# Recurrent entry on the unscaled sum, projections scaled by a row as their banks are read, and first units by part

## The chip, the cores and the metric

The kernel runs on one core of one Trainium2 chip. A core has TensorE (PE, which multiplies matrices into eight PSUM banks), ScalarE (ACT), VectorE (DVE), GpSimd (POOL) and SyncE (SP, which issues most transfers here). The metric is the device time of one execution, in microseconds (us). Times with a start are counted from the start of the profiled span.

## What is computed

A token block x of 256 tokens with 1024 features, in float32, goes through nine residual stages: feed-forward, the recurrent mixer ("even"), feed-forward, feed-forward, latent attention ("mla"), feed-forward, feed-forward, forgetting attention ("fox"), feed-forward. Each stage normalises x and adds its result to it. Cut to the parts that the change touches:

```
def _rmsnorm(x, gain):                     # x * rsqrt(mean(x*x)) * gain
def _swiglu(h, w_gate, w_up, w_down):      # D_FF = 2816
    return (silu(h @ w_gate) * (h @ w_up)) @ w_down
def _conv_rwkv_mixer(h, ...):              # stage 1, "even"
    p = h @ w_in                           # 3*512 conv columns, 3*512 + 32 + 32 + 96 recurrent ones
    gate_b, gate_c, h_in = split(p_conv)
    y_conv = gate_b * short_conv(gate_c * h_in, conv_w)          # 3 taps
    p_rwkv = p_rwkv + (shift(p_rwkv) - p_rwkv) * mu_shift        # the token before, mixed in
    r, k, v, dw, da, dg = split(p_rwkv)
    log_w = -softplus(-(w0 + tanh(dw) @ w_up)) - 0.5             # decay
    a = sigmoid(a0 + da @ a_up);  g = sigmoid(dg) @ g_up
    kk = normalised per head(k * k_k)
    y = scan over tokens: S = S*decay + (S@-kk)(kk*a) + v k ;  y_t = S@r_t
    y = group norm of y, bonus, times g
    return concat(y_conv, y) @ w_out
x = x + 0.5 * _swiglu(_rmsnorm(x, g[0]), ...)   # a feed-forward stage
x = x + mixer(_rmsnorm(x, g[1]))
```

## The kernel before

Every float32 operand of a product is split into a high part (rounded by a cast) and a low part (the rest), and a product is the sum of three: high by high, high by low, low by high (`three_products`, L385). Weights come from memory as units: `raw_gu` (1 MB) and `raw_dn` (0.5 MB). ACT makes the high parts (`hi_gu` L351, `hi_dn` L361), DVE or POOL the low parts (`lo_gu` L365, `lo_dn` L371, `lo_dn_pool` L378). A feed-forward stage has 22 units, the recurrent stage 12. Each engine's order is written out by hand; engines meet at semaphores, in the recurrent stage through `after(engine, other, step)`, which waits until the other engine has done the named step.

**An ordinary seam** (into stages 3, 5, 6, 8). DVE adds a stage's result to x in four quarters (L500). PE transposes the unscaled x (`gained_pe`, L456), ACT reads the banks scaled by the norm's gain into `h_hi` (L414), DVE makes `h_lo` (L442). The first unit runs on these: first the gate's column block by part of h, in the order `SEAM` (L399, L400 for high parts, L575 for low ones), then the up block with three products (L385). ACT squares x (L426, first half ahead of `h_hi`, second half behind it), takes the inverse root (L432, L435), DVE turns it into two diagonals (L465), PE multiplies them by ones into a bank (L474), ACT copies that: `rstd_row`, one factor per token in each column, by which gate and up are later scaled.

**The recurrent stage** is another thing at its entry: ACT squares x by quarters (L1019), POOL and ACT make the inverse root (L974, L1025 to L1037), DVE scales x by it (L1219), and only then PE transposes (L1414). So its 26 projection tiles (`tile(i)`, each 128 or 96 columns by 256 tokens, in three units' pieces) come out of their banks ready. For tiles 0 to 13, which are mixed with the token before, ACT reads the bank scaled by 1 - mu (`evac(i)`, L989) and DVE then adds mu times the bank shifted by a token (`mix(i)`, L1192). Tiles 14 to 25 are copied by ACT (`evac(i)`, L992): 14 to 17 are v, 18 to 25 the convolution's.

The chain of the stage: tiles 0 to 3 (k), their squares (L1048) and the key norm (PE L1445, DVE L1237, ACT L1060); tile 4 and 5 (low rank); tanh and two low-rank products (PE L1535, L1539), the gate's sigmoid (L1066), the decay's sigmoid (L1069) and the other one (`iclr`, L1072); the cumulative sum of the decays (PE L1547); kk, b, their scaled forms (DVE L1245 to L1254); key scores on PE (L1461); five levels of products that invert the chunk triangles (the first is PE L1505 at 246.63 us); states and outputs; group norm; the output products (`row` by `row`, L385, whose left operand is `h_both` from `conv_hi` L1152 and `conv_lo` L1378 for the convolution's half, with `y_conv` L1375 ahead).

Of the kernel before, what the change touches and what calls it, by code (L numbers as in the profile page):

```python
# [10 lines left out]
ALU = mybir.AluOpType  # L11
# [236 lines left out]
def build(nc, units_gu, units_dn, x_in, positions, constants, params, low_rank, final_gain, out, stages=STAGES):  # L248
# [6 lines left out]
    with ExitStack() as ctx:  # L255
# [30 lines left out]
        rstd_row = arena[:, 17, T:2 * T]  # L286
        banks = ctx.enter_context(nc.psum_tensor("banks", [P, 8, 512], F32))
# [37 lines left out]
        x_ready, stored = sem("x_ready"), sem("stored")  # L325
        first_gate_landed, first_gate = [sem("first_gate_landed_0"), sem("first_gate_landed_1")], sem("first_gate")
# [64 lines left out]
        SEAM = (("hi", 0), ("hi", 1), ("hi", 2), ("lo", 0), ("hi", 3), ("lo", 1), ("lo", 2), ("lo", 3))  # L391

# [5 lines left out]
        def high_products(out, w, h, first):  # L398
            nc.tensor.matmul(out, w[0], h, start=first, stop=False)  # L399
            return nc.tensor.matmul(out, w[1], h, start=False, stop=False)  # L400

# [65 lines left out]

        def rstd_row_pe(pe, s):

            if s == 0:  # L470
                pe.wait_ge(ones_loaded, 16)
            pe.wait_ge(diag_ready, ffn_index(s) + 1)
            for t in range(2):
                ins = nc.tensor.matmul(banks[:, 7, t * P:(t + 1) * P], const("ones"), rstd_diag[:, t, :], start=True, stop=True)  # L474
            ins.then_inc(row_summed, 1)

        def rstd_row_act(act, s):
            act.wait_ge(row_summed, ffn_index(s) + 1)
            nc.scalar.copy(rstd_row, banks[:, 7, 0:T]).then_inc(row_ready, 1)

        def ffn_index(s):
            return sum(k == "ffn" for k in stages[:s])
# [44 lines left out]
        FIRST_UP_BANK = 5  # L527
# [32 lines left out]
        def ffn_first_up(pe, s):  # L560
# [4 lines left out]
            gate, up = banks[:, bank, 0:T], banks[:, FIRST_UP_BANK if s == 0 else bank, T:2 * T]  # L565
# [29 lines left out]
            for part, b in SEAM:  # L595
                gate_part(part, b)
            for k in range(KD):
                w = slice((KD + k) * P, (KD + k + 1) * P)
                ins = three_products(up, (gu_hi[:, 0, w], gu_lo[:, 0, w]), (h_hi[:, k, :], h_lo[:, k, :]),
                                     k == 0, k == KD - 1)  # L600
            ins.then_inc(gu_used, 1)
# [102 lines left out]
        def ffn_all_act(act, s):  # L704
# [13 lines left out]
            else:  # L718
# [21 lines left out]
        def ffn_all_dve(dve, s):  # L740
# [24 lines left out]
            ffn_dve(dve, b, 0, f, True, None, seam_bank(s), FIRST_UP_BANK if s == 0 else None)  # L765
# [95 lines left out]
        def even_names():  # L861
# [9 lines left out]
            act = [("square_x", 0), ("square_x", 1), "ln_x0", "rstd_x0"] + evac(0, 4) + ["square_k"] + evac(4, 5) + ["ln_k"] + evac(5, 6) + ["tanh", "gate_sig"] + evac(6, 7)  # L871
            act += ["decay_sig", "iclr", "inv_k"] + evac(7, 8) + ["e0", "em", "e1", "mid", "factor", "gate"] + evac(8, 10)
            act += halves("m", -1) + evac(10, 11)
            for l in range(NL):
                act += ([("tok", TOKS[l])] if l < 3 else []) + [("mt", l)]
                act += (halves("m", l) if l < NL - 1 else []) + ["a_crossed"] * (l == 0) + evac(11 + l, 12 + l)
            act += [("tok", "v")] + evac(16, 17) + ["g"] + evac(17, 18) + ["uw"] + evac(18, 19) + ["phi"] + evac(19, 21) + ["y0"]
            act += evac(21, 24) + ["square_y"] + evac(24, 25) + ["ln_y"] + [("conv_hi", j) for j in range(3)] + ["rstd_y"]
            act += evac(25, 26) + [("conv_hi", 3)] + [("y_hi", j) for j in range(4)]
            mix = lambda a, b: [("mix", i) for i in range(a, b)]  # L880
            dve = [("scaled", t, c) for t in range(2) for c in range(2)] + ["omu", "omka"] + mix(0, 5) + ["one_row", "key_ss"] + mix(5, 8) + ["kkn", "b", "at", "bt"]
            dve += ["mt0", "mt1"] + mix(8, 9) + ["kh", "ab0", "ab", "kt"] + mix(9, 11)
            for l in range(NL):
                dve += halves("x", l) + ["ak"] * (l == 3) + [("mt", l)] + (["rt", "ec"], ["bonus"], [], [], ["rk"])[l]
                dve += mix(11 + l, 12 + l) if l < 3 else []
            conv = lambda j: [(n, j) for n in ("u", "tap0", "tap1", "tap2")]
            state = lambda n: [("sd", n), ("sum", n), ("s", n)]
            dve += ["rb", "bv", "bv_b", "uw", "s1"] + conv(0) + [("q", 0), ("q", 1)] + state(1) + [("y", 1)]
            dve += conv(1) + state(2) + [("y", 2)] + conv(2) + [("y", 3)] + conv(3) + ["centred"]
            dve += [("y_conv", j) for j in range(3)] + [("conv_lo", j) for j in range(3)] + [("y_conv", 3), ("conv_lo", 3)]  # L890
# [3 lines left out]
            pool = [("bias_x", 0), ("bias_x", 1), "pads"]  # L894
# [21 lines left out]
        x_ss, x_bias = mla_stats[:, 16:20], mla_stats[:, 20:22]  # L916
        x_scaled = [arena[:, slot, 0:D] for slot in (RC, VC)]
# [45 lines left out]

        def mix_column(i):
# [5 lines left out]
        def even_pool(pool, s):  # L970
            done = EV["pool"].done
            for t in range(2):
                after(pool, "act", ("square_x", t))
                done(nc.gpsimd.tensor_scalar(x_bias[:, t:t + 1], x_ss[:, 2 * t:2 * t + 1], 1.0 / D, NORM_EPS, ALU.mult, ALU.add),  # L974
                     ("bias_x", t))
# [3 lines left out]
        def even_act(act, s):  # L979
# [5 lines left out]
            def evac(i):  # L985
                after(act, "pe", ("tile", i))
                if i < MIXED:
                    m = 96 if i in LOW_TILES else P
                    ins = nc.scalar.activation(tile_target(i), tile_place(i), ACT.Copy,  # L989
# [2154 lines left out]
```

## Time and profile before

| what | value |
|---|---|
| median of 3 runs | 1494.03 us (1493.0 to 1494.61) |
| profiled execution, its own time | 1492.92 us |
| its span from first to last instruction | 1491.1 us |
| granted TensorE clock, mean | 0.999 |
| PE / weight loads / DVE / ACT / POOL busy | 99 / 86 / 67 / 57 / 34 % |
| recurrent stage, in the trace | from about 194 to about 354 us |

"Busy" is the share of the span in which an engine had an instruction under way; where matmuls overlap each other they are counted once, so 99% of PE doesn't say how fast it works. A wait of PE is told with the line that waited and the line that released it; these few waits, and the place of each in the program, are what an edit on another engine can shorten or lengthen.

### The profile page before, as it was taken

How to read it: one execution, taken by the hardware profiler on the slowest of the kernel's cores; microseconds unless marked ns; L12 is line 12 of the kernel's file. 1: busy time of each engine (PE TensorE's matmuls, PEld its weight loads, DVE VectorE, ACT ScalarE, POOL GpSimd, SP SyncE). 2: the span in 40 equal slices, each digit the busy share in tenths (PEclk: the TensorE clock that was granted, in tenths of full speed). 3: DMA queues.
4: the chain of work that ended last, by engine and by line, in shares of the span. 5: the costliest groups of instructions: out<-in, count | busy, mean ns of one | idle time of the engine just before them, and what ended most of it. 6: DMA issues, size and time to landing. Idle time of an engine off the chain costs nothing. (4 is left out here: it accounts for less than half of the span.)

```text
span 1491.1 us, 25605 instructions
## 1 busy us (share of the span) xinstructions
PE 1469.7 (99%) x9520; PEld 1275.5 (86%) x9520; DVE 1002.2 (67%) x1303; ACT 854.2 (57%) x1316; POOL 508.1 (34%) x207
## 2 busy tenths in 40 slices
PE   8999999999999999999999999999999999999998
PEld 7888889898888888888988888888888887888886
DVE  6776567568775567765665777557765589877654
ACT  5555576446555565555676555555555678655544
POOL 2444400001444335443441344334444300144442
PEclk9999999999999999999999999999999999999999
DMA  7655542235555545555533555545655453265552
GB/s 258 225 206 195 185 141 74 101 115 176 205 197 187 200 154 193 199 189 202 184 114 113 183 197 187 206 156 189 207 192 190 169 198 113 100 211 186 205 184 87
DMA packets 48812, 259.99 MB, mean 174 GB/s; under 512 B 5584, under 2 KB 5968, under 8 KB 28144
## 3 DMA queue, kind: packets, MB, share of 16 engines
q1 hardware_dynamic: 29520, 190.49, 36.1%
q10 hardware_dynamic: 19152, 68.53, 13.8%
q8 instruction: 42, 0.69, 0.2%
q14 instruction: 18, 0.15, 0.0%
q0 software_dynamic: 80, 0.14, 0.0%
HBM read 258.08 MB, written 1.05 MB: 174 GB/s over the span
## 5 line engine op out<-in xcount | busy, mean ns | idle before, releaser
L378 POOL TENSOR_TENSOR dn_lo<-raw_dn,dn_hi 128x1024 fp32r<-128x1024 f32 x138 | 472.6, 3425 | 837.5 <-ACT dn_hi L361 828.6
L365 DVE TENSOR_TENSOR gu_lo<-raw_gu,gu_hi 128x2048 fp32r<-128x2048 f32 x161 | 369.3, 2294 | 181.8 <-ACT gu_hi L351 180.1
L606 PE MATMUL banks<-h_both,gu_hi 128*128 128x512 f32 x2016 | 478.1, 389 | 0.0
L606 PEld LDWEIGHTS banks<-h_both,gu_hi 128*128 128x128 f32 x2016 | 378.0, 188 | 78.2
L351 ACT CAST gu_hi<-raw_gu 128x2048 fp32r<-128x2048 f32 x160 | 304.9, 1906 | 12.0 <-PE banks L385 12.0
L613 PEld LDWEIGHTS banks<-h_both,gu_lo 128*128 128x128 f32 x2016 | 258.5, 191 | 9.8
L613 PE MATMUL banks<-h_both,gu_lo 128*128 128x256 f32 x2016 | 261.5, 283 | 0.0
L385 PE MATMUL banks<-dn_hi,act_hi 128*128 128x512 f32 x528 | 207.3, 393 | 0.5 <-DVE act_lo L555 0.5
L385 PE MATMUL banks<-dn_lo,act_hi 128*128 128x512 f32 x528 | 207.0, 392 | 0.0
L385 PE MATMUL banks<-dn_hi,act_lo 128*128 128x512 f32 x528 | 205.5, 389 | 0.0
L547 DVE TENSOR_TENSOR silu<-silu,arena 128x256 f32<-128x256 f32 x126 | 175.2, 1391 | 4.3
L361 ACT CAST dn_hi<-raw_dn 128x1024 fp32r<-128x1024 f32 (+1 forms) x162 | 167.8, 1036 | 7.0 <-DMA raw_dn<-units_dn 3.7
L521 ACT ACTIVATE silu<-silu 128x256 f32<-128x256 f32 x132 | 55.2, 418 | 168.6 <-DVE silu L547 168.1
L517 ACT COPY arena<-banks 128x256 f32<-128x256 f32 x126 | 46.7, 371 | 177.8 <-PE banks L613 177.5
L544 DVE TENSOR_TENSOR silu<-banks,arena 128x256 f32<-128x256 f32 x126 | 53.1, 422 | 98.8 <-ACT arena L517 98.7
L385 PEld LDWEIGHTS banks<-dn_hi,act_lo 128*128 128x128 f32 x528 | 99.2, 188 | 21.8
L385 PEld LDWEIGHTS banks<-dn_hi,act_hi 128*128 128x128 f32 x528 | 99.6, 189 | 18.5 <-POOL dn_lo L378 0.7
L385 PEld LDWEIGHTS banks<-dn_lo,act_hi 128*128 128x128 f32 x528 | 99.7, 189 | 15.7
L555 DVE TENSOR_TENSOR act_lo<-act,act_hi 128x256 fp32r<-128x256 f32 x132 | 62.7, 475 | 62.4 <-ACT act_hi L523 62.4
L523 ACT CAST act_hi<-act 128x256 fp32r<-128x256 f32 x132 | 53.6, 406 | 71.3 <-DVE act L553 68.4
L385 PE MATMUL banks<-gu_hi,h_both 128*128 128x512 f32 (+2 forms) x292 | 92.7, 384 | 0.2
L519 ACT COPY arena<-banks 128x256 f32<-128x256 f32 x126 | 47.0, 373 | 62.3 <-PE banks L613 61.7
(386 smaller groups left out, 1562.7 us busy)
## 6 DMA issues: line engine op xcount, KB each, us to landing
raw_gu<-units_gu SPq DMA_DIRECT2D x161, 1024.0 KB, 4.8
raw_dn<-units_dn ACTq DMA_DIRECT2D x130, 512.0 KB, 3.5
raw_dn<-units_dn SPq DMA_DIRECT2D x32, 512.0 KB, 3.4
x<-x_in SPq DMA_DIRECT2D x2, 512.0 KB, 4.9
cst<-constants SPq DMA_DIRECT2D x1, 688.0 KB, 6.0
raw_gu<-units_gu SPq DMA_DIRECT2D x2, 256.0 KB, 6.3
raw_gu<-units_gu SPq DMA_DIRECT2D x1, 512.0 KB, 7.5
lora<-low_rank SPq DMA_DIRECT2D x1, 512.0 KB, 7.2
```

What stands on the lines that cost most here:

```text
L351: nc.scalar.copy(gu_hi[:, p, :], raw_gu[:, p, :]).then_inc(gu_hi_ready, 1)
L361: nc.scalar.copy(dn_hi[:, p, 0:n], raw_dn[:, p, 0:n]).then_inc(dn_hi_ready, 1)
L365: nc.vector.tensor_tensor(gu_lo[:, p, :], raw_gu[:, p, :], gu_hi[:, p, :].bitcast(F32), ALU.subtract).then_inc(gu_lo_ready, 1)
L378: nc.gpsimd.tensor_tensor(dn_lo[:, p, 0:n], raw_dn[:, p, 0:n], dn_hi[:, p, 0:n].bitcast(F32), ALU.subtract).then_inc(dn_lo_ready, 1)
L385: ins = nc.tensor.matmul(out, a, b, start=first and i == 0, stop=last and i == 2)
L521: nc.scalar.activation(silu[:, p, :], silu[:, p, :], ACT.Silu).then_inc(silu_ready, 1)
L523: nc.scalar.copy(act_hi[:, p, :], act32[:, p, :]).then_inc(act_hi_ready, 1)
L544: nc.vector.tensor_tensor(silu[:, p, :], banks[:, 2 * p, 0:T], lo_half[:, p, 0, :], ALU.add).then_inc(halves_added, 1)
L547: nc.vector.tensor_tensor(silu[:, p, :], silu[:, p, :], rstd_row, ALU.mult).then_inc(gate_ready, 1)
L555: nc.vector.tensor_tensor(act_lo[:, p, :], act32[:, p, :], act_hi[:, p, :].bitcast(F32), ALU.subtract).then_inc(act_lo_ready, 1)
L606: ins = nc.tensor.matmul(banks[:, 2 * p + side, :], gu_hi[:, p, w], h_both[:, k, :, :].rearrange("p i t -> p (i t)"), start=k == 0, stop=F ...
L613: ins = nc.tensor.matmul(banks[:, 2 * p + side, 0:T], gu_lo[:, p, w], h_hi[:, k, :], start=False, stop=k == KD - 1)
```

## The change

1. At the start DVE writes zeros into a slot, and PE runs nine 128x128 float32 products on them before its first wait for a transfer.
2. In the recurrent stage the scaling of x goes. `gained_pe` transposes the unscaled sum as at an ordinary seam; ACT's squares and root stand behind `h_hi`, and `rstd_row_pe` and `rstd_row_act` make the row (in bank 3, copied to a free slot, `even_row`). A new DVE step, `raw(i)`, reads each tile's bank times the row. Tiles 14 to 25 are done with that. For tiles 0 to 13 `evac` and `mix` now read what `raw` wrote. Twelve ACT copies and three POOL instructions go; 26 DVE instructions come.
3. ACT's cast `hi_gu` of unit 3 moves from behind `evac(7)` to right behind the gate's sigmoid and ahead of `evac(6)`; DVE's `lo_gu` of unit 3 moves from behind `bt` to ahead of `raw(6)`. `kh` stands earlier on DVE, `mix(10)` behind the first level's masks, `raw(24)` and `raw(25)` ahead of `y_conv`.
4. First units of stages 2, 3, 5, 6 and 8, and tiles 0 and 1 of the recurrent stage, go gate and up together, by part of h (`both_by_part`), up in a bank of its own. ACT does all of `h_hi` first, then both squares.

```diff
+        def both_by_part(pe, s, outs, w, summed=None):
+            for part in ("hi", "lo"):
+                for b in range(4):
+                    for k in part_of_h(pe, s, part, b):
+                        for side, out_ in enumerate(outs):
+                            weights = w((side * KD + k) * P)
+                            if part == "hi":
+                                high_products(out_, weights, h_hi[:, k, :], k == 0)
+                            else:
+                                ins = nc.tensor.matmul(out_, weights[0], h_lo[:, k, :], start=False, stop=k == KD - 1)
...
+            both_by_part(pe, s, (gate, up), lambda a: (gu_hi[:, 0, a:a + P], gu_lo[:, 0, a:a + P])).then_inc(gu_used, 1)
...
-                squares_act(act, s, 0, loaded=stages[s - 1] in ("mla", "fox"))
                 h_hi_act(act, s)
-                squares_act(act, s, 1)
+                for t in range(2):
+                    squares_act(act, s, t, loaded=True)
                 inverse_root_act(act, s)
...
             def evac(i):
-                after(act, "pe", ("tile", i))
-                if i < MIXED:
...
-                else:
-                    ins = cp(tile_target(i), tile_place(i))
+                after(act, "dve", ("raw", i))
+                m = 96 if i in LOW_TILES else P
+                done(nc.scalar.activation(tile_target(i), unmixed(i), ACT.Copy,
+                                          scale=omu[0:m, mix_column(i):mix_column(i) + 1]), ("evac", i))
...
             h_hi_act(act, s)
-            nc.scalar.preload_act_table(ACT.Ln)
+            for t in range(2):
+                squares_act(act, s, t, loaded=True)
+            inverse_root_act(act, s)
             hi_gu(act, *unit(s, 1))
+            rstd_row_act(act, s)
...
             done(nc.scalar.activation(low(0, GATE_RANK, 1), low(0, GATE_RANK, 1), ACT.Sigmoid), "gate_sig")
+            hi_gu(act, *unit(s, 3))
             evac(6)
             after(act, "pe", "decay_in")
...
+            def raw(i):
+                after(dve, "pe", ("tile", i))
+                place = tile_place(i)
+                done(tt(unmixed(i) if i < MIXED else tile_target(i), place, even_row[0:place.shape[0], :], ALU.mult), ("raw", i))
+
             def mix(i):
                 after(dve, "act", ("evac", i))
-                done(stt(out=dst[:, 1:T], in0=tile_place(i)[:, 0:T - 1], scalar=pcol("mu", mix_column(i), m), in1=dst[:, 1:T],
+                done(stt(out=dst[:, 1:T], in0=unmixed(i)[:, 0:T - 1], scalar=pcol("mu", mix_column(i), m), in1=dst[:, 1:T],
...
+            raw(5)
             mix(5)
             lo_dn(dve, *unit(s, 2))
+            lo_gu(dve, *unit(s, 3))
+            raw(6)
+            raw(7)
             mix(6)
             mix(7)
...
             lo_gu(dve, *unit(s, 9))
+            raw(24)
+            raw(25)
             for some in ((0, 1, 2), (3,)):
                 for j in some:
-                    after(dve, "act", ("evac", 22 + j))
                     own(("tap2", j))
+                    own(("raw", 22 + j))
                     done(tt(c4(YC)[:, j, :], c4(CB)[:, j, :], c4(CC)[:, j, :], ALU.mult), ("y_conv", j))
...
+            both_by_part(pe, s, (tile_place(0), tile_place(1)), lambda a: w(a, P), lambda ins: done(ins, ("tile", 0))
+                         ).then_inc(gu_used, 1)
+            tile(2)
+            rstd_row_pe(pe, s)
+            tile(3)
+            tile(4)
             after(pe, "act", "square_k")
...
+            nc.vector.memset(arena[:, 0, 0:2 * P], 0.0).then_inc(zeros_ready, 1)
...
+            pe.wait_ge(zeros_ready, 1)
+            for i in range(9):
+                nc.tensor.matmul(banks[:, 3, 0:P], arena[:, 0, 0:P], arena[:, 0, P:2 * P], start=True, stop=True)
             pe.wait_ge(ident_loaded, 16)
```

ACT's order in the recurrent stage, from the table for the gate's sigmoid to the cast of unit 3, before (L1066 is the gate's sigmoid, L1069 the decay's, L1072 `iclr`, L1077 the inverse norm):

```order
L1061 ACT_TABLE_LOAD
L989 ACTIVATE act<-banks,mla_stats 96x256
L1064 ACTIVATE act<-act 32x256
L1066 ACTIVATE act<-act 96x256
L989 ACTIVATE arena<-banks,mla_stats 128x256
L1069 ACTIVATE arena<-banks 128x1024
L1072 ACTIVATE arena<-banks,par 128x256 x4
L1075 ACT_TABLE_LOAD
L1077 ACTIVATE arena<-arena,eps_col 128x1024
L989 ACTIVATE arena<-banks,mla_stats 128x256
L351 CAST gu_hi<-raw_gu 128x2048
```

and after the change (L1057 the gate's sigmoid, L1061 the decay's, L1064 `iclr`):

```order
L1052 ACT_TABLE_LOAD
L1001 ACTIVATE act<-arena,mla_stats 96x256
L1055 ACTIVATE act<-act 32x256
L1057 ACTIVATE act<-act 96x256
L353 CAST gu_hi<-raw_gu 128x2048
L1001 ACTIVATE arena<-arena,mla_stats 128x256
L1061 ACTIVATE arena<-banks 128x1024
L1064 ACTIVATE arena<-banks,par 128x256 x4
```

The cast of unit 3 stood behind the last of them and now stands between the two sigmoids; the bank reads have become reads of the arena.

DVE's order from the key norm's maximum (L1237) to the first masks of key scores (L1196), before:

```order
L1237 TENSOR_SCALAR arena<-banks 128x1024
L1192 SCALAR_TENSOR_TENSOR act<-banks,par,act 96x255
L371 TENSOR_TENSOR dn_lo<-raw_dn,dn_hi 128x1024
L1192 SCALAR_TENSOR_TENSOR arena<-banks,par,arena 128x255 x2
L1245 SCALAR_TENSOR_TENSOR arena<-arena,par 128x256 x4
L1249 TENSOR_TENSOR arena<-arena 128x1024
L1251 SCALAR_TENSOR_TENSOR arena<-arena 128x1024
L1254 TENSOR_TENSOR arena<-arena 128x1024
L365 TENSOR_TENSOR gu_lo<-raw_gu,gu_hi 128x2048
L1196 TENSOR_TENSOR arena<-banks,cst 128x1024
```

and after (L1222 the maximum, L1174 `raw`, L1179 `mix`, L1183 the masks):

```order
L1222 TENSOR_SCALAR arena<-banks 128x1024
L1174 TENSOR_TENSOR arena<-banks,silu 96x256
L1179 SCALAR_TENSOR_TENSOR act<-arena,par,act 96x255
L373 TENSOR_TENSOR dn_lo<-raw_dn,dn_hi 128x1024
L367 TENSOR_TENSOR gu_lo<-raw_gu,gu_hi 128x2048
L1174 TENSOR_TENSOR arena<-banks,silu 128x256 x2
L1179 SCALAR_TENSOR_TENSOR arena<-arena,par 128x255 x2
L1234 SCALAR_TENSOR_TENSOR arena<-arena,par 128x256 x4
L1238 TENSOR_TENSOR arena<-arena 128x1024
L1240 SCALAR_TENSOR_TENSOR arena<-arena 128x1024
L1243 TENSOR_TENSOR arena<-arena 128x1024
L1245 TENSOR_TENSOR arena<-arena 128x1024
```

The low split of unit 3 now stands ahead of `raw(6)` and `raw(7)`, and `kh` (L1245) has come in front of the masks.

DVE's order at the end of the stage, before (L1368 centres the group norm, L1375 `y_conv`, L1378 `conv_lo`):

```order
L1368 SCALAR_TENSOR_TENSOR arena<-banks,arena 128x1024
L365 TENSOR_TENSOR gu_lo<-raw_gu,gu_hi 128x2048
L1375 TENSOR_TENSOR arena<-arena 128x256 x3
L1378 TENSOR_TENSOR h_both<-arena,h_both 128x256 x3
L1375 TENSOR_TENSOR arena<-arena 128x256
```

and after (L1376, L1385, L1388):

```order
L1376 SCALAR_TENSOR_TENSOR arena<-banks,arena 128x1024
L367 TENSOR_TENSOR gu_lo<-raw_gu,gu_hi 128x2048
L1174 TENSOR_TENSOR arena<-banks,silu 128x256 x2
L1385 TENSOR_TENSOR arena<-arena 128x256 x3
L1388 TENSOR_TENSOR h_both<-arena,h_both 128x256 x3
L1385 TENSOR_TENSOR arena<-arena 128x256
```

The two reads of tiles 24 and 25, which ACT did, stand ahead of `y_conv`.

## Rows read from the trace of the kernel before

**Rows 1.** The page, part 1: busy us (share), instructions.
```profile
PE 1469.7 (99%) x9520; PEld 1275.5 (86%) x9520; DVE 1002.2 (67%) x1303; ACT 854.2 (57%) x1316; POOL 508.1 (34%) x207
```

**Rows 2.** PE's waits: us in total, times, longest.
```profile
PE banks L1505 <- issue: 1.7, 1, 1.7
...
PE banks L385 <- DVE dn_lo L371: 0.2, 1, 0.2
```

**Rows 3.** Line L456, 0 to 10 us: ns min/median/max, first and last start.
```profile
L456 PE MATMUL banks<-cst,x x16: 421/421/476, 5.4 to 8.6; 128*128 128x128 f32 x16
```

**Rows 4.** Line L456, 190 to 1300 us.
```profile
L456 PE MATMUL banks<-cst,x x112: 270/273/330, 354.2 to 1299.9; 128*128 128x128 f32 x112
```

**Rows 5.** Timeline of the start (start us, us, instruction, [idle before]).
```profile
5.39 3.68 PE L456 MATMUL banks<-cst,x 128*128 128x128 f32 x16 [5.39 <-DMA cst<-constants]
...
7.91 3.03 ACT L414 ACTIVATE h_both<-banks,par 128x256 fp32r<-128x256 f32 x8 [4.96 <-PE banks L456]
...
22.07 0.19 PEld L385 LDWEIGHTS banks<-dn_hi,act_hi 128*128 128x128 f32 x1 [0.65 <-POOL dn_lo L378]
```

**Rows 6.** Timeline of PE at the recurrent stage's entry.
```profile
193.19 0.39 PE L385 MATMUL banks<-dn_hi,act_lo 128*128 128x512 f32 x1
...
195.63 2.13 PE L1414 MATMUL banks<-cst,arena 128*128 128x128 f32 x16 [2.05 <-DVE arena L1219]
...
198.13 0.35 PE L399 MATMUL banks<-h_both,gu_hi 128*128 128x256 f32 x1 [0.37 <-ACT h_both L414]
```

**Rows 7.** Timeline of PE and DVE at the seam into stage 3.
```profile
540.24 2.06 PE L456 MATMUL banks<-cst,x 128*128 128x128 f32 x16
...
542.06 0.36 PE L399 MATMUL banks<-h_both,gu_hi 128*128 128x256 f32 x1
542.26 0.28 PE L400 MATMUL banks<-h_both,gu_lo 128*128 128x256 f32 x1
542.38 0.28 PE L399 MATMUL banks<-h_both,gu_hi 128*128 128x256 f32 x1
...
547.31 0.47 DVE L465 TENSOR_SCALAR arena<-cst,rstd 128x128 f32<-128x128 f32 x2
...
548.39 0.61 PE L474 MATMUL banks<-arena,cst 128*128 128x128 f32 x4
```

**Rows 8.** Groups of lines, 190 to 354 us: busy us, mean ns | idle before.
```profile
L365 DVE TENSOR_TENSOR gu_lo<-raw_gu,gu_hi 128x2048 fp32r<-128x2048 f32 x12 | 27.4, 2285 | 2.9 <-ACT gu_hi L351 2.9
...
L989 ACT ACTIVATE arena<-banks,mla_stats 128x256 f32<-128x256 f32 x12 | 5.7, 476 | 6.9 <-PE banks L385 6.9
L1192 DVE SCALAR_TENSOR_TENSOR arena<-banks,par,arena 128x255 f32<-128x255 f32 x12 | 5.7, 479 | 11.4 <-ACT arena L989 11.4
...
L992 ACT COPY arena<-banks 128x256 f32<-128x256 f32 x12 | 4.5, 371 | 22.3 <-PE banks L385 22.2
```

**Rows 9.** Timeline: a DVE product of a bank and the row, first stage.
```profile
18.79 0.42 DVE L538 TENSOR_TENSOR silu<-banks,arena 128x256 f32<-128x256 f32 x1
```

**Rows 10.** Timeline of PE: key norm, low-rank product, cumulative sum.
```profile
213.10 1.88 PE L1445 MATMUL banks<-arena,cst 128*128 128x512 f32 x4
...
220.60 0.69 PE L1535 MATMUL banks<-lora,act 64*128 64x512 f32 x1
...
225.50 3.61 PE L1547 MATMUL banks<-cst,arena 128*128 128x256 f32 x16
```

**Rows 11.** Timeline of ACT: decay sigmoid, cast of unit 3.
```profile
222.62 1.03 ACT L1069 ACTIVATE arena<-banks 128x1024 f32<-128x1024 f32 x1 [1.44 <-PE banks L1539]
...
227.82 1.89 ACT L351 CAST gu_hi<-raw_gu 128x2048 fp32r<-128x2048 f32 x1
```

**Rows 12.** Timeline: first level; end of the recurrent stage, DVE and PE.
```profile
246.63 1.16 PE L1505 MATMUL banks<-arena 64*64 64x64 f32 x64 [0.61 <-DVE arena L1206]
...
331.57 1.09 DVE L1378 TENSOR_TENSOR h_both<-arena,h_both 128x256 fp32r<-128x256 f32 x3 [2.04 <-ACT h_both L1152]
...
332.37 0.40 PE L385 MATMUL banks<-dn_hi,h_both 128*128 128x512 f32 x1
```

More of the change, by code:

```diff
@@ L478, in rstd_row_act @@
             act.wait_ge(row_summed, ffn_index(s) + 1)
[L479 removed]
+            nc.scalar.copy(even_row if stages[s] == "even" else rstd_row, banks[:, row_bank(s), 0:T]).then_inc(row_ready, 1)
         def ffn_index(s):
[L482 removed]
+            return sum(k in ("ffn", "even") for k in stages[:s])
         def add_to_x(dve, s):
@@ L875, in even_names @@
                 act += ([("tok", TOKS[l])] if l < 3 else []) + [("mt", l)]
[L876 to L879, printed above, removed]
+                act += (halves("m", l) if l < NL - 1 else []) + ["a_crossed"] * (l == 0) + (evac(11 + l, 12 + l) if l < 3 else [])
@@ L880, in even_names @@
+            act += [("tok", "v"), "g", "uw", "phi", "y0", "square_y", "ln_y"] + [("conv_hi", j) for j in range(3)] + ["rstd_y"]
+            act += [("conv_hi", 3)] + [("y_hi", j) for j in range(4)]
             mix = lambda a, b: [("mix", i) for i in range(a, b)]
-            dve = [("scaled", t, c) for t in range(2) for c in range(2)] + ["omu", "omka"] + mix(0, 5) + ["one_row", "key_ss"] + mix(5, 8) + ["kkn", "b", "at", "bt"]
-            dve += ["mt0", "mt1"] + mix(8, 9) + ["kh", "ab0", "ab", "kt"] + mix(9, 11)
+            raw = lambda *places: [("raw", i) for i in places]
@@ L891, in even_names @@
+            dve += [("q", 0), ("q", 1)] + state(1) + raw(20) + [("y", 1)]
+            dve += conv(1) + state(2) + raw(21) + [("y", 2)] + conv(2) + raw(22) + [("y", 3)] + conv(3) + raw(23) + ["centred"]
+            dve += raw(24, 25) + [("y_conv", j) for j in range(3)] + [("conv_lo", j) for j in range(3)] + [("y_conv", 3), ("conv_lo", 3)]
             for j in range(4):
@@ L1078, in even_act @@
             evac(7)
-            hi_gu(act, *unit(s, 3))
             after(act, "pe", "cumsum")
@@ L1254, in even_dve @@
             done(tt(flat(BT_), flat(BT_), flat(EM), ALU.mult), "bt")
-            lo_gu(dve, *unit(s, 3))
+            after(dve, "act", "factor")
+            done(tt(flat(KH), flat(KC), flat(AI), ALU.mult), "kh")
+            raw(8)
             after(dve, "pe", "ab")
@@ L1271, in even_dve, with raw_and_mix @@
             lo_dn(dve, *unit(s, 3))
-            mix(10)
-            level(0)
+            def raw_and_mix(i):
+                raw(i)
+                mix(i)
+            level(0, lambda: raw_and_mix(10))
             own(("mix", 9))
@@ L1296, in even_dve, with lo_and_raw @@
             level(3, ak)
-            level(4, lambda: lo_dn(dve, *unit(s, 5)))
+            def lo_and_raw():
+                lo_dn(dve, *unit(s, 5))
+                raw(14)
+            level(4, lo_and_raw)
             after(dve, "pe", "rk")
@@ L1336, in convolution @@
                 u, y = u_conv[:, j, :], c4(CC)[:, j, :]
-                after(dve, "act", ("evac", 18 + j))
+                own(("raw", 18 + j))
                 done(tt(u[:, 2:258], y, u[:, 2:258], ALU.mult), ("u", j))
@@ L1423, in tile @@
                 if ks[0] == 0 and i >= 6:
-                    after(pe, *(("dve", ("mix", i - 2)) if i - 2 < MIXED else ("act", ("evac", i - 2))))
+                    after(pe, "dve", ("raw", i - 2))
                 m = 96 if i in LOW_TILES else P
```

137 lines of the change are left out of this document (45 added, 92 removed).

## Prediction

> **What bounds the kernel now.** I began with the page: TensorE (PE) is busy for 1469.7 of 1491.1 us [rows 1]. An edit elsewhere can only pay if PE waits for that work, and costs if it makes PE wait. So the next view is PE's own waits [rows 2], then PE's timeline at the places the diff touches: the start [rows 5], the entry of the recurrent stage [rows 6], an ordinary first unit [rows 7], the joins inside the recurrent stage [rows 10, 12] and its end [rows 12]. For each place I ask which engine delivers last before and after.
>
> **What a step costs here.** In the recurrent stage, 190 to 354 us: one scaled bank read on ACT 0.476 us, one mix on DVE 0.479, one plain bank copy on ACT 0.371, one low split of a whole unit on DVE 2.29 [rows 8]. The new DVE instruction, a bank times a row, 128x256, has a twin in the feed-forward stage: 0.42 us [rows 9]. Twenty-six of them are 10.9 us of DVE; the twelve ACT copies that go are 4.5 us. Neither sum is the answer, since DVE and ACT idle before most of these. A 256-column matmul comes every 0.12 us (542.26, 542.38 [rows 7]); this is how I turn counts into time (estimate; 48 of them, 5.76 us).
>
> The Trainium skill, page "VectorE: DVE Perf Modes", section "Specifications", says that VectorE sits closer to SBUF and ScalarE closer to PSUM, which speaks against moving these bank reads. The rows give 0.42 against 0.371 us for the same shape; the trace agrees in direction, by 0.05 us. By the page alone no sum could be made.
>
> **Part 1, zeros at the start.** PE is idle for 5.39 us and then does 16 transposes at 421 ns each [rows 3, 5]; the same instruction is 273 ns later in the program [rows 4], and starts every 0.115 us rather than 0.23 us (3.68 us for 16 against 2.06 [rows 5, 7]). The nine matmuls fit into the idle 5.39 us. If they bring the later rate, the last transpose is some 1.6 us earlier, and ACT's h_hi (7.91) some 1 us. What follows does not follow: the gate's low weights and DVE's h_lo stand behind DVE's own splits. What can profit is ACT's chain to PE's first down product, before which the weight load waits 0.65 us [rows 5]. I take -0.4, bounds 0 and -0.65.
>
> The Trainium skill, page "TensorE: Matmul & The Clock Gate", section "Part 4: PE-mode transpose", says that the full clock does not engage for transposes. By that rule the 16 would stay as they are and this term would be 0. The trace speaks against it: the granted clock is given as full in both places, yet 421 ns and 273 ns stand for the same instruction.
>
> **Part 2, entry of the recurrent stage.** Before, the last down product starts at 193.19, PE waits 2.05 us for the scaled x, transposes from 195.63, and starts the first tile at 198.13 [rows 6]. After, the entry is like an ordinary seam: there transposes follow the last product at once, and the first product comes 1.82 us after the first transpose [rows 7]. Counted from 193.42 (0.23 behind the start of the last product, the pace of 512 columns), that is 195.24: 2.9 us gained, and taking tiles 0 and 1 together saves some 0.6 of small waits for h parts. It does not last, because the row must now exist before any tile leaves its bank. The low split of unit 1 (2.29, behind h_lo, a down split and the diagonals) ends at about 204.3 on DVE, an estimate, the row's matmuls and its copy give the row at about 204.85. From there the chain to the key norm is raw 0 and 1, evac 1, mix 1, a down split, raw 2, evac 2, a gate-up cast on ACT, evac 3, mix 3, a square: 0.84 + 0.48 + 0.48 + 1.2 + 0.42 + 0.48 + 1.9 + 0.48 + 0.48 + 0.5 = 7.3, with ten hand-overs 0.5 more: 212.65, against 213.10 before [rows 10]. PE, being early, waits there about 2.6 us. Then low split 2.29, raw 4, evac 4, mix 4, the norm's maximum, the table, evac 5 and tanh bring the low-rank product to 220.8, before 220.60 [rows 10]. **Entry gain 0.**
>
> **Part 3, the split moved behind the gate.** ACT before: gate sigmoid, evac 6, decay sigmoid at 222.62, and the cast hi_gu(3) only at 227.82 [rows 11]. After, hi_gu(3) stands right behind the gate sigmoid: from about 221.0 to 223.1. DVE then does lo_gu(3), 2.29 us, to 225.5, and only then raw 6, 0.42, which evac 6 on ACT waits for. The decay sigmoid stands behind evac 6 in ACT's order although its own input is ready by then: evac 6 at 225.9, the sigmoid 0.35 behind its start as ACT's instructions overlap, 226.25 instead of 222.62. The inverse root and evac 7 move with it, and so do the kk products of DVE. The cumulative sum on PE starts at 225.50 before [rows 10], some 0.4 after its input; after, at 228.76: **+3.26**, of which PE shows about 3.05 as one wait. The key scores come 3.6 later, as their chain has no such 0.4. PE's later waits of 0.2 and 0.61 us [rows 2, 12] go, since DVE had the time: the first level product moves from 246.63 to 249.4, **+2.75** in all. DVE has lost the split of 2.29 from behind bt, so it is not the bound.
>
> In the levels, raw, evac and mix stand in a row where evac and mix stood: 0.42 more in a chain that PE mostly covers by weight products; I take **+0.2** over three levels (0 to 1.26, all three in full).
>
> **Part 4, end of the stage.** Before, the three y_conv lie ready, conv_lo starts on DVE at 331.57 and PE goes from tile 25 into the row product at 332.37 [rows 12]. After, DVE must read tile 25 from its bank (raw 25) before the y_conv. Tile 25 ends at 332.37; then raw 0.42, a y_conv (DVE takes 1.09 for three of this shape [rows 12]), conv_hi, conv_lo: the row product at about 334.45, **+2.1**. ACT's evac 24 and 25 go, but ACT was not late. Bounds: 0.4 (a row product needs only j = 0 to start, and PE finds other work) and 2.6.
>
> **Part 5, ordinary first units.** Transposes at 540.24, first product 542.06, 48 products until the row's matmuls start at 548.39 [rows 7]: 0.57 us above 48 x 0.12. By part, PE has eight products for each 0.76 us in which ACT makes a pair of h_hi, so it is not starved. But the row also waits for DVE's diagonals, 547.31 to 547.78 [rows 7]. Both give 547.8: **-0.55** for each of stages 3, 5, 6 and 8, -2.2 in all (bounds: 0, if the diagonals slip as the squares now stand behind h_hi, to -2.4). For stage 2, behind the recurrent stage, ACT's second cast decides; I take -0.1 (0 to -0.55). ACT's squares and root move behind h_hi; they are covered by DVE's low split up to 547.3, and cost up to the 1.1 us of one square if that cover is gone.
>
> **Sum.** -0.4 + 0 + 2.75 + 0.2 + 2.1 - 2.2 - 0.1 = +2.35 us. The profiled execution took 1492.9 us, so 1495.3; the median of the runs shown is 1494.03, 1.1 above it, so **1496.4 us**.
>
> **Rivals.**
> (A) Forecast, likeliest, own range +0.4 to +3.8: chance 0.52.
> (B) PE's 1.7 us of "issue" at L1505 [rows 2], in which it waits for nothing that the profile shows, goes with the moved instructions, for their number before it changes. For: it is a place, not a dependency. Against: levels have the same instructions after. +0.65, 1494.7: 0.13.
> (C) The two new waits, 2.6 and 3.05 us, slow PE afterwards as the 5.4 us did at the start, 1.84 us for 16 transposes. For: rows 3. Against: the 2.05 us wait at 195.63 did not; 16 transposes took 2.13 us [rows 6], and 3.05 is nearer to it than to 5.39. It would add about 1.9: 1498.3, slower: 0.12. It decides if a wait of 3 us is enough.
> (D) The other side: DVE and ACT are ahead at the gate. Were raw 6 ready before hi_gu(3) matters, or the entry's lead kept through the key norm, then of the +2.75 at most 0.3 stays; and were raw 25 covered by remaining weight products, +0.4 in place of 2.1. Then -0.4 + 0.3 + 0.2 + 0.4 - 2.3 = -1.8, and with half of the entry's 3.5 kept, about -3.6: 1490.5, faster. For: 2.9 us are gained at the entry. Against: ACT's order puts the decay sigmoid behind evac 6. 0.12.
> (E) Both chains cost more: levels 1.26, end 2.6, seams 0. +2.35 + 1.1 + 0.5 + 2.2 = +6.1: 1500.1, slower: 0.11.
>
> **Range and chances.** 0.2% (3.0 us) is about what a measurement can tell from no change. From 1492.2 to 1499.2 holds A, B, most of C and the nearer part of D. Faster 0.12 (D), same 0.60 (most of A, B, a part of D), slower 0.28 (C, E and A's upper end).
>
> **What would show it.** In the trace after: a PE wait at the key norm of some 2.6 us and one before the cumulative sum of some 3, the latter released by ACT's iclr with DVE's lo_gu and raw 6 before evac 6; a PE wait of about 2 us behind tile 25 for h_both; transposes at the start of 270 to 330 ns; the row's matmuls 0.5 us sooner at the seams. I am wrong if the low-rank product comes well before 220 us, if tiles leave their banks before the row exists, or if the seams show new waits for the diagonals.

## The result, and the profile after

The changed kernel takes 1497.18 us (median of 14 executions, 1495.18 to 1499.94), the one before 1493.72 us (1492.40 to 1494.61). The ratio is 1.0026 (95% interval 1.0017 to 1.0034): slower by a quarter of a per cent, 3.5 us between the medians and 3.9 by the ratio. The predicted time was 1496.4 us. The profiled execution of the changed kernel took 1498.03 us, 0.85 above its median. Three single executions in the experiments below (5188.03, 3457.8 and 1614.11 us) lie far outside the others of their kernels and are left out of every median, range and ratio.

PE's waits in the changed kernel (us in total, times, longest):

```profile
PE banks L1447 <- ACT arena L1039: 2.6, 1, 2.6
PE banks L1545 <- ACT arena L1064: 2.2, 1, 2.2
PE banks L387 <- DVE h_both L1388: 1.9, 1, 1.9
PE banks L3106 <- DVE arena L3091: 1.2, 1, 1.2
...
PE banks L1507 <- issue: 0.7, 1, 0.7
```

The first three are new waits in the recurrent stage: the key norm, the cumulative sum, and the output products behind tile 25. They are those that the prediction named, with 2.6, 3.05 and about 2. The fourth is PE's wait at the start for DVE's zeros. The "issue" wait of [rows 2] is 0.7 instead of 1.7.

Timeline of the changed kernel at the gate, ACT, DVE and PE, and PE's first output product:

```profile
221.13 1.88 ACT L353 CAST gu_hi<-raw_gu 128x2048 fp32r<-128x2048 f32 x1
...
223.04 2.29 DVE L367 TENSOR_TENSOR gu_lo<-raw_gu,gu_hi 128x2048 fp32r<-128x2048 f32 x1 [1.14 <-ACT gu_hi L353]
...
225.25 0.42 DVE L1174 TENSOR_TENSOR arena<-banks,silu 128x256 f32<-128x256 f32 x1
...
225.71 0.51 ACT L1001 ACTIVATE arena<-arena,mla_stats 128x256 f32<-128x256 f32 x1 [2.69 <-DVE arena L1174]
...
226.12 1.00 ACT L1061 ACTIVATE arena<-banks 128x1024 f32<-128x1024 f32 x1
...
228.63 5.41 PE L1545 MATMUL banks<-cst,arena 128*128 128x256 f32 x16 [2.22 <-ACT arena L1064]
...
337.70 0.50 PE L387 MATMUL banks<-dn_hi,h_both 128*128 128x512 f32 x1 [1.85 <-DVE h_both L1388]
```

Read from top to bottom it is a chain: cast of unit 3, its low split, the read of tile 6, evac 6, the decay's sigmoid at 226.12 (222.62 before, [rows 11]), and PE at 228.63 (225.50 before, [rows 10]). The row of the cumulative sum has one thing more: 16 products take 5.41 us, where the same 16 took 3.61. The last row is PE's wait for tile 25's read and what hangs on it.

Windows of PE in the changed kernel: stretch, PE's busy time (x), granted clock, DMA share, GB/s.

```profile
210.00:214.00 4.00, 1.65 (x2) 0.72 0.27 109
214.00:218.00 4.00, 4.00 (x24) 0.85 0.70 242
226.00:230.00 4.00, 1.78 (x8) 0.86 0.75 262
230.00:234.00 4.00, 4.00 (x15) 0.72 0.00 0
...
338.00:342.00 4.00, 4.00 (x12) 0.57 0.03 9
```

At each of the three waits the granted clock falls from 2.4 to 1.2 GHz (0.50 in the single microseconds 213, 230 and 340) and comes back. Added up over windows of one microsecond each fall lasts 3.4 us: the first begins while PE still waits for the key norm (granted clock 0.89 in microsecond 211), the other two just after PE has started again. Before the change the clock is 1.00 over 200 to 350 us. Timeline of the changed kernel at the start and at the seam into stage 3:

```profile
5.18 2.81 PE L470 MATMUL banks<-cst,x 128*128 128x128 f32 x16
...
21.65 0.47 PE L387 MATMUL banks<-dn_hi,act_hi 128*128 128x512 f32 x1
...
547.00 2.10 PE L470 MATMUL banks<-cst,x 128*128 128x128 f32 x16
...
554.68 0.66 PE L492 MATMUL banks<-arena,cst 128*128 128x128 f32 x4
```

The first down product comes at 21.65, where it was 22.10 before. From the first transpose to the row's matmuls the seam takes 7.68 us, 8.15 before [rows 7].

### The profile page after: what moved, and what is told of

The parts are those of the page before. It is cut to its first block and busy times, and to the rows that moved or that the text cites. A ratio compares the mean times of both kernels' runs of the same rounds, so it can differ in the third digit from the quotient of the medians.

```text
span 1496.2 us, 25653 instructions
## 1 busy us (share of the span) xinstructions
PE 1475.4 (99%) x9542; PEld 1281.7 (86%) x9542; DVE 1014.9 (68%) x1329; ACT 847.3 (57%) x1298; POOL 506.3 (34%) x205
## 5 line engine op out<-in xcount | busy, mean ns | idle before, releaser
L564 DVE TENSOR_TENSOR silu<-silu,arena 128x256 f32<-128x256 f32 x126 | 180.3, 1431 | 4.3
```

Source lines behind the costliest of these rows:

```text
L564: nc.vector.tensor_tensor(silu[:, p, :], silu[:, p, :], rstd_row, ALU.mult).then_inc(gate_ready, 1)
```

## Experiments

All are told by their ratio to the kernel before, timed on the same chip; "better than the change" is a difference of two such ratios, in us. "Theory 1" below is order plus clock, "theory 2" order alone, "theory 3" the number of reads.

**The split put back.** ACT's cast of unit 3 behind evac 7 again, DVE's low split behind `bt`:

```diff
-            hi_gu(act, *unit(s, 3))
             evac(6)
...
             evac(7)
+            hi_gu(act, *unit(s, 3))
...
-            lo_gu(dve, *unit(s, 3))
             raw(6)
...
             done(tt(flat(BT_), flat(BT_), flat(EM), ALU.mult), "bt")
+            lo_gu(dve, *unit(s, 3))
```

> The changed kernel (median 1497.2 us) with the high and low split of unit 3 put back where they stood before: ACT's cast behind evac 7, DVE's low split behind bt. Theory 1 (order plus clock): PE's wait of 2.22 us before the cumulative sum goes, with 0.4 us of slack more (about -2.75), and so does the low clock that follows it in the trace, which takes 1.9 us of PE time (228.9 to 232.8 us at half of full speed): 1492.5 us, and the profile shows the decay sigmoid within 0.5 us of the low-rank product's end and no PE wait over 0.5 us at the cumulative sum. Theory 2 (order alone, the low clock is paid for by slack): 1494.4 us. Theory 3 (the 26 new DVE reads are what costs): within 1 us of 1497.2.

Measured: ratio 1.0013 (1.0005 to 1.0022), median 1495.3 us, 1.9 us better than the change. The wait at the cumulative sum is gone (226.32 us). That is less than either theory gave: the first level starts at 245.25 us against 242.62 before (these are its first products; the 246.63 us given above for the kernel before is its second product), since PE now waits for the split of unit 3 and for `copy_m`, which stands behind evac 9 and so behind the new read of tile 9. Theory 3, which gave no gain over 1 us, has the median and the trace against it, though the intervals of the two ratios just touch (1.0017 to 1.0022). The profile has one fall of the clock, at the key norm; the wait of 1.9 us behind tile 25 is still there, and in this execution no fall follows it (windows of PE, columns as above):

```profile
330.00:338.00 8.00, 6.15 (x36) 1.00 0.45 131
338.00:342.00 4.00, 4.00 (x19) 1.00 0.41 135
```

**Tile 25's read late.**

```diff
             raw(24)
-            raw(25)
             for some in ((0, 1, 2), (3,)):
+                if some == (3,):
+                    raw(25)
                 for j in some:
```

> The changed kernel with the bank read of tile 25 moved behind the first three y_conv and conv_lo on DVE. Theory 1 (order plus clock): PE's wait of 1.85 us behind tile 25 goes and with it the low clock of 337.9 to 341.8 us, 1.9 us of PE time: 1497.2 - 1.9 - 1.9 = 1493.4 us, and no wait over 0.3 us for h_both in the profile. Theory 2 (order alone): 1495.3 us. Theory 3 (the number of DVE reads costs): 1497.2 us, with the wait in another place.

Measured: 1.0018 (1.0009 to 1.0026), median 1496.0 us, 1.2 us better than the change, with intervals that overlap. The wait for h_both is gone, as expected; the size is below both theories, and its profile shows why one execution can't be read alone. The wait at the key norm is the same 2.56 us, but this time no fall follows, so PE is at the cumulative sum earlier and waits 3.0 us there, and the fall there is twice as long, 6.8 us by windows of one microsecond. One more, of 3.4 us, follows the "issue" wait, here 1.96 us, which ends at 278.5 us. Windows of PE:

```profile
210.00:214.00 4.00, 1.97 (x6) 1.00 0.20 76
214.00:218.00 4.00, 4.00 (x36) 1.00 0.76 262
226.00:230.00 4.00, 1.68 (x4) 0.70 0.74 262
230.00:234.00 4.00, 4.00 (x10) 0.50 0.00 0
```

From the cumulative sum to the key scores PE takes 11.26 us in it, 9.94 in the changed kernel, 8.14 before.

**Both.**

> Both edits of the two runs before together: split of unit 3 back, tile 25's read late. Theory 1 (order plus clock): 1492.5 + 1493.4 - 1497.2 = 1488.7 us; the only clock fall left in the recurrent stage is the one at the key norm, so the mean granted clock is 0.997 or more. Theory 2 (order alone): 1492.5 us. Theory 3 (DVE reads cost): over 1496 us.

Measured: 1.0000 (0.9991 to 1.0009), median 1492.54 us. Taking the two edits back makes up for the whole loss of 3.9 us. That is less than theory 2 gave (4.7 us, 1497.2 to 1492.5) and less than half of theory 1's 8.5; the median meets theory 2's figure only because the kernel before is faster on this chip (1492.96 us, 1493.72 in the first comparison). Alone, too, each edit was worth less than either theory said. What is left in the trace is a recurrent stage 2 us longer than before (stage 2's first transposes at 356.12 us, 354.16 before), with one fall of the clock, at the key norm; the seams pay for it.

**Waits filled.** Products of the identity by itself, in banks written over later, ahead of the three waits; nothing is taken away.

```diff
+            for _ in range(11):
+                mm(banks[:, 1, 0:P], ident, ident, start=True, stop=True)
             after(pe, "act", "square_k")
             over_heads("key_norm", INV, 6)
...
+            after(pe, "dve", "key_ss")
+            for _ in range(10):
+                mm(banks[:, 6, 0:P], ident, ident, start=True, stop=True)
             after(pe, "act", "iclr")
...
             tile(25, range(4, KD))
+            for _ in range(8):
+                mm(banks[:, 4, 0:P], ident, ident, start=True, stop=True)
```

A first version wrote the fillers of the key norm into bank 6 as well, where nothing ordered them behind DVE's earlier read of that bank; it has no measured time. This was expected of it:

> The changed kernel, with products of the identity by itself put in front of PE's three waits (11 before the key norm, 10 before the cumulative sum, 8 behind tile 25, 0.23 us each at full clock), into banks that are written over later. They add work that nobody reads and take no dependency away; they only keep PE busy where it waited. Theory 1 (the idle stretches cost a second time through the clock): the granted clock stays full through 200 to 350 us, the last two falls are saved whole and the first partly: 1493 us (1492 to 1495). Theory 2 (the waits alone cost, the low clock is slack): 1497.2 us or up to 1 us above it, for fillers that last longer than a wait.

And of the version that ran:

> The changed kernel, with products of the identity by itself put in front of PE's three waits (11 before the key norm, 10 before the cumulative sum, 8 behind tile 25, 0.23 us each at full clock), into banks that are written over later. They add work that nobody reads and take no dependency away; they only keep PE busy where it waited. The changed kernel has a ratio of 1.0026 to the one before, and its profiled execution shows three stretches of some 4 us at half clock behind these waits. Theory 1 (idle stretches are paid a second time through the clock, in most executions): full clock through 200 to 350 us, ratio 1.0005 to 1.0015, two falls of 1.9 us saved, if they happened in each execution. Theory 2 (the waits alone cost, the low clock is slack): 1.0026 or up to 0.0005 above it, for fillers that last longer than a wait.

Measured: 1.0003 (0.9994 to 1.0013), median 1494.1 us and its executions lie within 1493.81 to 1494.33, where the changed kernel has 1495.18 to 1499.94. So 29 products that nobody reads (58 instructions of PE in the profile, 9600 for 9542) make the kernel 3.4 us faster. Timeline, then windows of PE:

```profile
209.36 2.62 PE L1527 MATMUL banks<-cst 128*128 128x128 f32 x22
212.09 1.98 PE L1447 MATMUL banks<-arena,cst 128*128 128x512 f32 x4
...
228.37 3.72 PE L1550 MATMUL banks<-cst,arena 128*128 128x256 f32 x16 [0.73 <-ACT arena L1064]
```

```profile
226.00:230.00 4.00, 3.27 (x23) 1.00 0.76 264
230.00:234.00 4.00, 4.00 (x21) 1.00 0.01 2
...
338.00:342.00 4.00, 4.00 (x20) 1.00 0.40 131
```

The key norm comes at the same time as with the wait (212.35), the cumulative sum too (228.63); what follows is at full clock, 3.72 us for the 16 products in place of 5.41. Theory 2 falls: the low clock is paid for. Not all of the 3.4 us need be the clock. Stage 2's first transposes come at 356.95 us, 361.24 in the changed kernel's profile; of these 4.3 us the two later falls are 3.1 (the pairs of stretches are given below, in the account of the sum), 0.7 is the "issue" wait, which is absent here, and the rest is small.

**Read of tile 6 first.** The change's order at the gate, with one line moved, and tile 25's read late:

```diff
             lo_dn(dve, *unit(s, 2))
-            lo_gu(dve, *unit(s, 3))
             raw(6)
+            lo_gu(dve, *unit(s, 3))
             raw(7)
```

> The changed kernel with tile 25's read late and one line moved at the gate: DVE's read of tile 6 ahead of, not behind, the low split of unit 3, which else stays where the change put it. If the fault of the change's order was only that evac 6, and with it the decay sigmoid, stood behind that split: the decay sigmoid starts where it did with the split put back (223.6 us), and since the split is no longer behind bt either, the masks of the key scores start 2.3 us earlier and PE's three waits of 0.44, 0.43 and 0.75 us between 237 and 246 us mostly go: ratio 0.9990 (0.9980 to 0.9998), against 1.0000 with the split put back. If the split itself is what delays (ACT's cast before the decay sigmoid): 1.0005 or more.

Measured: 0.9981 (0.9972 to 0.9990), median 1490.6 us. ACT and DVE in it:

```profile
221.16 0.41 DVE L1174 TENSOR_TENSOR arena<-banks,silu 128x256 f32<-128x256 f32 x1
...
222.38 2.29 DVE L367 TENSOR_TENSOR gu_lo<-raw_gu,gu_hi 128x2048 fp32r<-128x2048 f32 x1 [0.80 <-ACT gu_hi L353]
...
222.66 1.01 ACT L1061 ACTIVATE arena<-banks 128x1024 f32<-128x1024 f32 x1
```

The decay's sigmoid is back at 222.66 us (222.62 before) and the first level at 243.07. So the split can stand right behind the gate's sigmoid; the fault was one read on the wrong side of it. Against the kernel that differs from this one by that line alone (tile 25's read late, 1.0018) this is 0.0037 better, 5.5 us, the wait at the cumulative sum is 0.16 us instead of 2.97, and the profile has no fall of the clock in the recurrent stage. Beside the kernel with both edits taken back it is 0.0019 better. Of the three waits named in the expectation 0.47 us is left, before the first level.

**Reordered entry.** That kernel, and the chain to the low-rank product in another order (the moved lines alone, ACT's then DVE's):

```diff
             hi_dn(act, *unit(s, 1))
+            evac(2)
+            evac(3)
...
             square_k(1)
-            evac(2)
-            hi_gu(act, *unit(s, 2))
-            evac(3)
             square_k(2)
             done(square_k(3), "square_k")
+            hi_gu(act, *unit(s, 2))
+            evac(4)
             hi_dn(act, *unit(s, 2))
-            evac(4)
...
             raw(0)
             raw(1)
+            raw(2)
             mix(0)
             mix(1)
-            lo_dn(dve, *unit(s, 1))
-            raw(2)
             raw(3)
             mix(2)
             mix(3)
-            lo_gu(dve, *unit(s, 2))
+            lo_dn(dve, *unit(s, 1))
             raw(4)
+            after(dve, "pe", "key_norm")
+            done(ts(split2(flat(INV)), two(6), 1e-24, None, ALU.max), "key_ss")
+            lo_gu(dve, *unit(s, 2))
             mix(4)
...
-            after(dve, "pe", "key_norm")
-            done(ts(split2(flat(INV)), two(6), 1e-24, None, ALU.max), "key_ss")
             raw(5)
...
             mix(8)
+            raw(9)
             own("kh")
...
-            raw(9)
             done(tt(flat(KT_), flat(KH), flat(EM), ALU.mult), "kt")
```

> The kernel of the run before, and the chain to the low-rank product put in an order that lets the entry's lead through: ACT does evac 2 and 3 and the four squares before the cast of unit 2; DVE reads tiles 2 and 3 early, and takes the key norm's maximum ahead of the low split of unit 2; the read of tile 9 stands ahead of the masks of ab. Theory (the lead of some 3 us at the entry was lost to the order between entry and low-rank product, not to the number of reads): key norm without a wait over 0.3 us at about 210 us, low-rank product at 217.5 us (221.4 in the changed kernel), no low clock there, ratio 0.9965 (0.9950 to 0.9980). Rival (the 26 reads are too much for DVE, which is then late with its splits): low-rank product after 220 us or waits for gu_lo of together over 2 us, ratio no better than the run before.

Measured: 0.9957 (0.9943 to 0.9970), median of five 1487.1 us, faster than both kernels. Timeline of PE:

```profile
209.75 1.98 PE L1448 MATMUL banks<-arena,cst 128*128 128x512 f32 x4
...
215.24 0.51 PE L387 MATMUL banks<-h_both,gu_hi 128*128 128x256 f32 x2 [0.69 <-DVE gu_lo L367]
...
218.31 0.69 PE L1534 MATMUL banks<-lora,act 64*128 64x512 f32 x1
```

The key norm follows tile 4 without a wait, the low-rank product comes at 218.31 (expected 217.5; 220.60 before), and the clock is 1.00 throughout the stage. All 26 reads are still on DVE, so their number is not what made the change slower.

**Seams alone**, on the kernel before: `both_by_part` in stages 2, 3, 5, 6 and 8 and both squares behind `h_hi`, as in the change's diff, with up in a bank of its own and ACT's table loaded ahead of `h_hi`; nothing else.

> The kernel before, with the first units of stages 2, 3, 5, 6 and 8 by part and the squares behind h_hi, and nothing else of the change. The prediction's term: -0.55 us for each of stages 3, 5, 6, 8 and -0.1 for stage 2, ratio 0.9985 (0.9982 to 0.9990), each seam 0.5 us shorter from its first transpose to the next stage's. If the diagonals slip with the squares: 0.9995 to 1.0005, and PE waits for the diagonals.

Measured: 0.9987 (0.9978 to 0.9996), -1.9 us; the interval covers the predicted -2.2. From a seam's first transpose to its row takes 7.59 to 7.70 us, 8.11 to 8.21 before. The recurrent stage here is that of the kernel before, and its profile has something that bears on the prediction: the same wait of 2.06 us at the stage's entry, and this time a fall of the clock behind it (timeline, then windows of PE):

```profile
195.53 3.01 PE L1424 MATMUL banks<-cst,arena 128*128 128x128 f32 x16 [2.06 <-DVE arena L1229]
```

```profile
196.00:197.00 1.00, 1.00 (x8) 0.75 0.00 0
197.00:198.00 1.00, 1.00 (x7) 0.50 0.00 0
198.00:199.00 1.00, 1.00 (x6) 0.50 0.00 0
199.00:200.00 1.00, 1.00 (x7) 0.54 0.00 0
```

The 16 transposes take 3.01 us, where they took 2.13 before [rows 6].

**Without the zeros**, on the reordered kernel, and that kernel once more beside it:

```diff
-            pe.wait_ge(zeros_ready, 1)
-            for i in range(9):
-                nc.tensor.matmul(banks[:, 3, 0:P], arena[:, 0, 0:P], arena[:, 0, P:2 * P], start=True, stop=True)
             pe.wait_ge(ident_loaded, 16)
```

> The reordered kernel (ratio 0.9957 to the one before, its executions within 1.2 us of each other) without the nine products of zeros at the start. The prediction's term for them is 0.4 us (0 to 0.65): 1487.1 + 0.4 = 1487.5 us, transposes at the start at 421 ns again and PE's first down product 0.4 us later (21.65 us in the changed kernel, 22.10 in the one before). If the low clock at the start costs more than the transposes: over 1488.2 us. If nothing: within 0.15 us.

> The reordered kernel once more, beside the one without zeros on the same chip, so that the two can be compared and its ratio stands on more executions: 0.9957 (0.9948 to 0.9966).

Measured: 0.9970 (0.9958 to 0.9981) without them, 0.9962 (0.9948 to 0.9975) with them. The 0.8 us between the medians point the right way but lie inside both intervals: inconclusive as a time, so the predicted 0.4 us stands on the traces alone. These show the local effect: PE's first down product at 21.85 us without the zeros, at 21.60 with them in the profile beside it and at 21.72 in the first profile of that kernel. Transposes of the start without and with the zeros:

```profile
5.14 3.68 PE L470 MATMUL banks<-cst,x 128*128 128x128 f32 x16 [5.14 <-DMA cst<-constants]
```

```profile
5.17 2.23 PE L470 MATMUL banks<-cst,x 128*128 128x128 f32 x16 [0.19 <-DMA cst<-constants]
```

## Why the prediction was right, and where it was not

**The start**, predicted -0.4: 22.10 to 21.65 in the trace, -0.45, and the 0.65 us in front of PE's weight load are 0.24. In part it is luck: the transposes change rate in the middle (2.81 us for 16, not the 2.06 that was reckoned with), and that decides nothing, as PE then waits for DVE's low gate weights as the prediction said. The rule of the Trainium skill, page "TensorE: Matmul & The Clock Gate", section "Part 4: PE-mode transpose", that full clock does not engage for transposes doesn't hold here: 16 of them take 3.68 us or 2.23, by whether nine products stand ahead of them, and 3.01 or 2.13 by whether a fall of the clock follows the wait at the recurrent stage's entry.

**The entry**, predicted 0: key norm 212.35 for 212.65, wait 2.56 for 2.6, low-rank product 221.35 for 220.8. The low-rank product would have been half a microsecond early without the clock: where no fall followed the same wait (tile 25's read late) it is 220.30. That the order and not the number of reads eats the lead is shown by the reordered kernel.

**The gate**, predicted +3.26 at the cumulative sum: +3.13, by the very rows that the prediction listed. PE's wait there is 2.22 us and not 3.05, since the fall at the key norm has made PE late. The key scores were to be 3.6 late and are 4.93 late, the second product of the first level (246.63 before) 2.75 and is 4.18; the fall of the clock between them is the difference. With the waits filled the two are 3.22 and 2.46 late.

**The end of the stage**, predicted +2.1: the wait is 1.85 us. But the stretch that it ends has not grown: from the first level to the output products it takes 89.71 us, wait included, and took 89.75 before. The "issue" wait shrank from 1.7 to 0.7 us and the 0.6 and 0.2 us of [rows 2, 12] went. Of these the prediction had spent the last two in its +2.75. Counted from the second product of the first level, as it counts, the rest of the stage is 86.89 us, 85.74 before: +1.15 for the levels and the end together, predicted +2.3, and 85.97, +0.23, with the waits filled. So rival B held in part, though not for its reason: the same wait is 1.3 to 2.2 us in seven other kernels of this study, which have the moved instructions or have not, and absent in the filled one, whose instructions at that place are the same. Two profiled executions of one kernel, the reordered one, have 1.3 and 2.0. What it depends on stays open.

**Ordinary seams**, predicted -2.2 and -0.1: from one stage's transposes to the next's the changed kernel saves 0.32 us in stage 2, 0.46 in stage 3; seams alone measure -1.9. Right.

**The sum.** The forecast is 0.8 us from the median, and that is in part luck, for two errors of opposite sign meet in it. The sum has no fall of the clock, and without falls it is too high. Up to stage 2's first transposes its terms add up to +4.65 us (-0.4 + 0 + 2.75 + 0.2 + 2.1); with the waits filled and no fall PE is there at 356.95 us, +2.79 on 354.16, and nearly all of the difference are the levels and the end, above. Over the whole kernel filled is 1.0003, +0.4 us, where the sum has +2.35. The kernel before has falls too in some executions, which makes the +0.4 look small: beside its eight executions with a mean clock of 0.999 on that chip (1492.37 to 1493.07) filled, at 1494.1, is 1.1 to 1.8 us longer, still less than 2.35. The one execution of the changed kernel with 0.999 took 1495.18 us.

The other error is the clock, some 3 us of the measured 3.5 to 3.9. Rival C was true as a mechanism and had a chance of 0.12 as an alternative. That is the step that failed: "the 2.05 us wait at 195.63 did not" slow what followed was taken as evidence against a fall after 2.6 or 3.05 us, and a fall was treated as a yes or no for all executions. The row is read rightly, but it is one execution: in the profile of the seams alone the same wait is followed by a fall. The wait of 2.56 us at the key norm has a fall in three profiled kernels (the change, the split put back, both) and none in two (tile 25's read late, read of tile 6 first); 1.85 us behind tile 25 has one in the changed kernel and none with the split put back.

A fall is 3.4 us at half clock, once 6.8, and one of 3.4 costs 1.5 to 1.7 us where PE is the bound (cumulative sum to key scores 9.94 us against 8.49 filled; output products to the next transposes 23.54 against 21.89). It costs little at the key norm, where PE's time was slack before the cumulative sum (wait 2.22 us with the fall, 3.0 without). The 1.9 us per fall in the expectations of the first runs, from windows of some 4 us, was too much.

The chances should have had a term "one or two falls in most executions, +1.5 to +3", not "falls: yes or no". With it the forecast is about 1498 us, and slower by over 0.2% the likelier side. The prediction gave that side 0.28 and the same within 0.2% 0.60; measured is 1.0026 (1.0017 to 1.0034).

## What to carry to other kernels

When a read, a cast or a split is moved on one engine, ask what stands behind it in that engine's order whose own input is ready: here one instruction of 0.42 us on the wrong side of a split of 2.29 us cost 5.5 us, while the 26 new instructions stand in the fastest kernel of this study too. An idle stretch of PE (falls were seen at waits of 1.6 to 3.0 us here) can have two prices where PE bounds the kernel, the wait and, in some executions, the clock after it; filling it with work that nobody reads shows in one run about how much of a loss is the second, if the other waits are looked at beside it. A gain at the entry of a chain arrives only if every link up to PE's next wait moves with it: list them before counting it.

## What was not expected of the hardware

That the clock falls in some executions of a kernel and not in others, at one and the same wait; what decides it no run here shows. Times and mean clocks often go together: seams alone has six executions at 1490.5 to 1491.6 us with mean clocks of 0.997 to 0.999 and four at 1492.6 to 1493.2 with 0.996. Its profiled execution, one of the four, has two falls, the one at the stage's entry and one behind its "issue" wait of 1.6 us (granted clock 0.83 over 270 to 280 us). The reordered kernel has no fall in one profile and one in the other, behind its "issue" wait of 2.0 us (0.79 over 270 to 278 us). The kernel before is no exception: beside the filled kernel its executions at 0.999 have a median of 1492.6 us, those at 0.997 one of 1494.4, and on another chip the two groups overlap. In the filled kernel the spread is 0.5 us.
